# Eight late modulation blocks: from TensorE products to VectorE products with a TensorE sum over partitions

## The reference, cut to what matters

```
mod = silu(cond) @ w_ada + b_ada              # (1024) @ (1024 x 6144), for each of 2 conditioning vectors
sh1, sc1, g1, sh2, sc2, g2 = split(mod, 6)
h   = LN0(x) * (1 + sc1) + sh1                # needs the first third of mod
qkv, gates = h @ w_in                         # 1024 x 6656
x   = LN1(alpha * x + g1 * (merged @ w_o))    # needs the rest of mod, much later
```

## Time and profile before

| | |
|---|---|
| median of 3 runs | 1319.49 us (1319.38 to 1319.76) |
| profiled execution: its own time | 1320.33 us |
| profiled execution: span in the trace | 1317.9 us |
| TensorE busy | 1245.7 us (95% of the span) |
| VectorE busy | 947.4 us (72%) |
| ScalarE busy | 657.6 us (50%) |
| GpSimd busy | 235.2 us (18%) |
| granted TensorE clock, mean | 0.977 of full |

### The profile page before, as it was taken

How to read it: one execution, slowest core, us unless ns; L and a number is a source line. 1 busy time by engine, 2 the same in 40 slices (tenths; PEclk the granted TensorE clock), 3 DMA queues, 4 the chain that set the end, 5 groups by cost and what they waited for, 6 DMA issues and landing times.

```text
span 1317.9 us, 20584 instructions
## 1 busy us (share of the span) xinstructions
PE 1245.7 (95%) x6739; PEld 1009.7 (77%) x6739; DVE 947.4 (72%) x1714; ACT 657.6 (50%) x1043; POOL 235.2 (18%) x347
## 2 busy tenths in 40 slices
PE   7999999999999899998998999997899999999994
PEld 4677777778888799887876788784688888888862
DVE  5665531848461789888877524788999999999967
ACT  1522222232222688776763212224588888888843
POOL 0024441021242000011111001101131112112111
PEclk9999999999999999998998999997999999999997
DMA  9988995572655476532004533537999999999955
GB/s 349 281 299 276 289 290 217 167 238 82 221 168 207 164 232 218 182 140 81 25 24 128 183 131 105 203 144 263 322 387 374 372 389 381 384 384 377 376 218 119
DMA packets 152835, 309.46 MB, mean 235 GB/s; under 512 B 20700, under 2 KB 31516, under 8 KB 152760
## 3 DMA queue, kind: packets, MB, share of 16 engines
q1 hardware_dynamic: 122456, 233.24, 49.6%
q0 software_dynamic: 24384, 70.00, 17.4%
q10 hardware_dynamic: 5920, 5.24, 1.3%
HBM read 259.24 MB, written 61.24 MB: 243 GB/s over the span
## 4 chain that ended last, share of the span: by engine, by line
PE 81%; DVE 11%; issue 3%; DMA 2%; ACT 2%; SPq 1%; POOL 0%; DVEq 0%; ACTq 0%; POOLq 0%
PE psum_pair L1804 9%; PE psum_pair L1806 8%; PE psum_pair L1805 8%; PE psum_pair L1904 6%; PE psum_pair L2096 5%; PE psum_pair L2098 5%; PE psum_pair L2097 5%; PE psum_pair L1971 4%; PE psum_pair L1915 4%; PE psum_pair L1972 4%; PE psum_pair L1973 4%; PE psum_pair L1930 3%; PE psum_pair L2111 3%; PE psum_pair L2113 3%; PE psum_pair L2112 3%
## 5 line engine op out<-in xcount | busy, mean ns | idle before, releaser
L1804 PE MATMUL psum_pair<-w_parts,h_hi 128*128 128x512 f32 x520 | 206.5, 397 | 3.0 <-DVE h_lo L1313 3.0
L1806 PE MATMUL psum_pair<-w_parts,h_lo 128*128 128x512 f32 x520 | 203.4, 391 | 0.0
L1805 PE MATMUL psum_pair<-w_parts,h_hi 128*128 128x512 f32 x520 | 203.2, 391 | 0.0
L1164 DVE TENSOR_TENSOR w_parts<-w_raw,w_parts 128x1024 fp32r<-128x1024 f32 x72 | 83.4, 1220 | 97.3 <-ACT w_parts L878 96.8
L1018 ACT ACTIVATE p_unnormed<-psum_pair,minus_max 128x640 f32<-128x640 f32 (+1 forms) x160 | 113.4, 711 | 59.1 <-DVE minus_max L1391 58.9
L1391 DVE TENSOR_REDUCE minus_max<-psum_pair 128x1 f32<-128x640 f32 (+1 forms) x160 | 111.7, 715 | 22.6 <-PE psum_pair L1904 20.5
L1904 PE MATMUL psum_pair<-k_bundle,q_bundle 128*128 128x320 f32 (+1 forms) x576 | 115.7, 326 | 12.2 <-ACT p_unnormed L1018 10.8
L1804 PEld LDWEIGHTS psum_pair<-w_parts,h_hi 128*128 128x128 f32 x520 | 98.0, 188 | 25.1 <-issue 5.6
L1806 PEld LDWEIGHTS psum_pair<-w_parts,h_lo 128*128 128x128 f32 x520 | 98.0, 189 | 21.0
L1805 PEld LDWEIGHTS psum_pair<-w_parts,h_hi 128*128 128x128 f32 x520 | 98.2, 189 | 19.6
L1904 PEld LDWEIGHTS psum_pair<-k_bundle,q_bundle 128*128 128x128 f32 x576 | 86.2, 190 | 27.1 <-issue 24.8
(11 more groups left out here) (363 smaller groups left out, 2666.0 us busy)
## 6 DMA issues: line engine op xcount, KB each, us to landing
w_raw<-in_w_gate_up SPq DMA_DIRECT2D x76, 512.0 KB, 11.0
w_raw_c<-in_w_gate_up SPq DMA_DIRECT2D x72, 512.0 KB
w_raw_b<-in_w_down SPq DMA_DIRECT2D x72, 512.0 KB
w_raw<-in_w_in SPq DMA_DIRECT2D x52, 512.0 KB, 11.1
ada_raw<-in_w_ada SPq DMA_DIRECT2D x32, 512.0 KB, 9.3
k_transposed<-turned_staging POOLq DMA_DIRECT2D x48, 256.0 KB, 7.5
k_bundle<-k_transposed SPq DMA_DIRECT2D x14, 768.0 KB, 8.1
q_transposed<-turned_staging POOLq DMA_DIRECT2D x40, 256.0 KB, 6.3
```

The costliest lines, as they stand in the source:

```text
L1164: dve.tensor_tensor(w_parts[b % 2][:, 1, c], w_raw[:, c], w_parts[b % 2][:, 0, c].bitcast(F32), ALU.subtract).then_inc(lo_done, 1)
L1804: pe.matmul(out, a_hi, hi, start=kk == 0, stop=False)
L1805: pe.matmul(out, a_hi, lo, start=False, stop=False)
L1806: return pe.matmul(out, a_lo, hi, start=False, stop=kk == KD - 1)
```

## The change

The eight late `ada` units become two sums (after blocks 6 and 11). Their products are taken by VectorE, piece by piece: 32 pieces of 512 KB (`late_products`), each of four instructions on 128 x 512 values, which add up in `ada_acc`, four accumulators with two conditioning vectors each. TensorE multiplies the finished accumulators with a one-hot operand (`one_row`), which only sums over the partitions. The pieces are spread over blocks 3 to 11 as 3, 6, 6, 1, 1, 3, 5, 5, 2 (`LATE_CHUNKS`); pieces 0 to 15 make the first sum, 16 to 31 the second. Within a block, piece j of `count` is done at the end of VectorE's work for unit `j * 5 // count`. The ring of raw pieces shrinks from four places of a whole unit to two single pieces: SyncE issues piece m + 2 when VectorE has used piece m, behind the weights of its loop's turn. Pieces 0, 4, 8 and 12 of each sixteen belong to accumulator 0 and so on; the first two instructions of the first four pieces of each sixteen are plain products (`tensor_scalar`), all others are `scalar_tensor_tensor`, product and sum.

```diff
--- before.py
+++ after.py
@@ -204,21 +204,29 @@
 
         def ada_place(ci, c):
 
-            if ci < 4:
-                return ada_early[:, ci % 2, c], ada_early_in[ci % 2][c], 16 * (ci // 2 + 1)
-            return ada_ring[:, c], ada_in[c], 16 * (ci - 3)
+            return ada_early[:, ci % 2, c], ada_early_in[ci % 2][c], 16 * (ci // 2 + 1)
 
         KINDS = ["q", "q", "k", "k", "v", "v", "bq", "bq", "bkv", "g", "g", "g", "g"]
+        LATE_CHUNKS = {3: 3, 4: 6, 5: 6, 6: 1, 7: 1, 8: 3, 9: 5, 10: 5, 11: 2}
+        SUM_UNITS = {6: 7, 11: 11}
         units = []
         for b in range(NB - 6):
             _, i = blocks[b]
             if i == 2:
                 units += [("ck", None, 0, NT), ("ck", None, 1, NT), ("cbk", None, 0, NT)]
             units += [(KINDS[i], b, i, tt) for tt in range(NT)]
-            if b < N_ADA - 4:
-                units.append(("ada", -1, 4 + b, 0))
+            if b in SUM_UNITS:
+                units.append(("ada", -1, SUM_UNITS[b], 0))
         units = [("ada", -1, ci, 0) for ci in range(4)] + units
         N_EARLY = 4
+        late_of = {i: [] for i in range(len(units))}
+        m = 0
+        for b, count in LATE_CHUNKS.items():
+            of_block = [i for i, u in enumerate(units) if u[1] == b]
+            for j in range(count):
+                late_of[of_block[j * NT // count]].append(m)
+                m += 1
+        N_LATE = m
 
 
         pj_no, n = {}, 0
@@ -308,8 +316,9 @@
         vst_total = list(count)
 
         ada_early_in = [[sem(f"ada_early_in{i}_{c}") for c in range(NC_CH)] for i in range(2)]
-        ada_in = [sem(f"ada_in{c}") for c in range(NC_CH)]
+        ada_in = [sem(f"ada_in{c}") for c in range(2)]
         ada_used = sem("ada_raw_used")
+        acc_used = sem("ada_products_summed")
         mod_summed = sem("mod_summed")
         early_done = sem("picks_and_turned_bias_built")
         mod_done = sem("mod_columns_done")
@@ -327,7 +336,8 @@
         s3a = ExitStack()
         bundles = [(0, h) for h in range(A_HEADS)] + [(1, g) for g in range(B_KV)]
         sr = ExitStack()
-        ada_ring = sb("ada_raw", [P, NC_CH, 2, CW], F32, sr)
+        ada_ring = sb("ada_raw", [P, 2, 2, CW], F32, sr)
+        ada_acc = sb("ada_products", [P, 4, 2, CW], F32, sr)
         sr.close()
         qtb = [sb("q_bundle0", [P, REP, NT * P], F32R, s3a)]
         ktb = [sb("k_bundle0", [P, 2, 2, KCOL], F32R, s3a)]
@@ -338,6 +348,7 @@
         h_hi = sb("h_hi", [P, KD, NT * P], F32R, s12)
         h_lo = sb("h_lo", [P, KD, NT * P], F32R, s12)
         mod_parts = sb("mod_parts", [P, 2, CW], F32, s12)
+        one_row = mod_parts[:, 0, 0:34]
         cond_cols = sb("cond_columns", [P, KD, 32], F32, s12)
         bias12 = sb("ada_bias", [N_ADA, CW], F32, s12)
         cache = sb("cache_k", [P, D + B_KV * HD], F32, s12)
@@ -751,12 +762,14 @@
             def ada_weights(ci):
                 if 2 <= ci < 4:
                     sp.wait_ge(pj_ready, pj_no[ada_unit[ci - 2]] + 1)
-                if ci > 4:
-                    sp.wait_ge(ada_used, ci - 4)
                 for c in range(NC_CH):
                     dst, done, _ = ada_place(ci, c)
-                    src = ada_chunk(ci, c) if ci < 4 else ada_chunk(4 * (ci // 4) + c, ci % 4)
-                    sp.dma_start(dst, src).then_inc(done, 16)
+                    sp.dma_start(dst, ada_chunk(ci, c)).then_inc(done, 16)
+
+            def late_chunk(m):
+                if m >= 2:
+                    sp.wait_ge(ada_used, m - 1)
+                sp.dma_start(ada_ring[:, m % 2], ada_chunk(4 + 4 * (m // 16) + m % 4, m // 4 % 4)).then_inc(ada_in[m % 2], 16)
 
             for tt in range(NT):
                 src = t["x_prompt"][0] if tt == PROMPT else t["x_sample"][0, tt * P:(tt + 1) * P]
@@ -778,9 +791,15 @@
                 sp.dma_start(dst, t["ln2_b"][0:1, :].to_broadcast([P, D])).then_inc(out_cleared, 16)
             weights(1)
             for b in range(2, NB - 4):
-                if b - 2 < N_ADA - 4:
-                    ada_weights(b + 2)
                 weights(b)
+                if b == min(LATE_CHUNKS) + 1:
+                    late_chunk(0)
+                    late_chunk(1)
+                for i, u in enumerate(units):
+                    if u[1] == b - 2:
+                        for m in late_of[i]:
+                            if m + 2 < N_LATE:
+                                late_chunk(m + 2)
                 if b == 2:
                     sp.wait_ge(h_done, KD)
                     sp.wait_ge(cache_in, 112)
@@ -1268,7 +1287,7 @@
                 elif ci % 4 == 3:
                     r = ci // 4 - 1
                     dve.wait_ge(cache_in, 112 + 16 * (N_ADA - 4))
-                    dve.wait_ge(ada_used, ci - 3)
+                    dve.wait_ge(acc_used, r + 1)
                     dve.tensor_tensor(mst[:, r], mod_sum(r), bias_late[:, r], ALU.add).then_inc(mod_summed, 1)
 
 
@@ -1303,6 +1322,26 @@
                 dve.tensor_copy(h_mod[:, k], turned(n)[:, 0:NT * P]).then_inc(tr_free[n % 2], 1)
             for i in range(N_EARLY):
                 after(i)
+            link(dve.memset(one_row, 0.0))
+            link(dve.memset(one_row[:, 1:2], 1.0))
+
+            def late_products(m):
+                g, pair_of_k = m % 4, m // 4 % 4
+                dve.wait_ge(ada_in[m % 2], 16 * (m // 2 + 1))
+                if m == 16:
+                    dve.wait_ge(acc_used, 1)
+                for k in range(2):
+                    for s in range(2):
+                        acc, c = ada_acc[:, g, s], cond_t[:, 2 * pair_of_k + k, s:s + 1]
+                        if k == 0 and pair_of_k == 0:
+                            last = dve.tensor_scalar(acc, ada_ring[:, m % 2, k], c, None, ALU.mult)
+                        else:
+                            last = dve.scalar_tensor_tensor(acc, ada_ring[:, m % 2, k], c, acc, ALU.mult, ALU.add)
+                    if k == 0:
+                        link(last)
+                last.then_inc(ada_used, 1)
+                dve.wait_ge(ada_used, m + 1)
+
             for c in range(NC_CH):
                 dve.wait_ge(hi_done, c + 1)
                 dve.tensor_tensor(w_parts[0][:, 1, c], w_raw[:, c], w_parts[0][:, 0, c].bitcast(F32),
@@ -1322,6 +1361,8 @@
                     gain_tables()
                 if i - 2 >= N_EARLY:
                     after(i - 2)
+                for m in late_of[i]:
+                    late_products(m)
             after(len(units) - 2)
             after(len(units) - 1)
 
@@ -1769,14 +1810,13 @@
                 if b is None:
                     return
                 if kind == "ada" and ci >= 4:
-                    for k in range(2):
+                    r = ci // 4 - 1
+                    pe.wait_ge(ada_used, 16 * (r + 1))
+                    for s in range(2):
                         for g in range(4):
-                            src, done, value = ada_place(ci, g)
-                            if k == 0:
-                                pe.wait_ge(done, value)
-                            last = pe.matmul(mod_sum(ci // 4 - 1)[32 * g:32 * g + 32], cond_cols[:, 2 * (ci % 4) + k], src[:, k],
-                                             start=ci % 4 == 0 and k == 0, stop=ci % 4 == 3 and k == 1)
-                    last.then_inc(ada_used, 1)
+                            last = pe.matmul(mod_sum(r)[32 * g:32 * g + 32], one_row[:, 1 - s:33 - s], ada_acc[:, g, s],
+                                             start=s == 0, stop=s == 1)
+                    last.then_inc(acc_used, 1)
                     return
                 n = pj_no[i]
                 wait_bank(n)
@@ -2239,7 +2279,7 @@
                 if i == last_g:
                     for s in range(TST):
                         pool.wait_ge(tst_st[s], tst_total[s])
-                    pool.wait_ge(ada_used, N_ADA - 4)
+                    pool.wait_ge(acc_used, 2)
                     load_qk(pool, 0, first_in)
                     load_v(pool, 0, first_in)
             after(len(units) - 2)
```

## The result

The kernel after takes 1342.19 us in the median (1339.77 to 1347.39, four runs), the kernel before 1319.62 us in the same session: ratio 1.0173, 95% interval 1.0153 to 1.0194. It is slower, as forecast, but by 22.6 us where 10.8 were forecast, and it lies above the range. The profiled execution took 1347.39 us, its span is 1345.0 (before: 1317.9).

What follows compares the result with a forecast made beforehand. The prediction took TensorE to set the projection's pace, with VectorE's slack uneven. Its terms, -12.3 + 9.4 + 3.95 + 9.55 + 0.2 = +10.8 us, gave 1331.1 us profiled, 1330.3 on the median; range 1314 to 1338.

Steps and rivals of the forecast that it cites:

- Six units leave TensorE: Projection: eight late units go and two sums come, 6 x 2.05 = 12.3 us gained, all on the path.
- Block 8: Block 8: three pieces in units 0, 1 and 3 exceed VectorE's slack, so TensorE waits 3.95 us.
- The places named: Projection: TensorE idle about 9 us in block 6, 4 in 8, 9 to 10 in 10; none in 0 to 5, 7, 9, 11.
- the small things: Two memsets ahead of block 0 cost 0.2 us; SyncE's weights and GpSimd's wait for the second sum cost 0.
- The rival that held landings to be free: Projection: pieces land in 6.2 us or less throughout, sum +0.65, 1320.1 us; chance 0.20.
- A piece of four two-input products: VectorE: four instructions at 0.605 us with two waits of 0.12, 2.66 us a piece.
- the cheap piece: VectorE: a piece with two plain products, taken at 0.45 us each, costs 2.3 us; eight pieces are of this kind.
- Blocks 9 and 10: Block 9's landings leave VectorE a lag of 7.95 us; with block 10's pieces TensorE waits 9.55 us.
- block 6's landing: Blocks 4 and 5, ahead of block 6: five rounds of landings taken as 11, 8 and three of 5.5 us, 35.5 in all.
- a lag of 6.7: Block 6: VectorE ready for its first unit after 58.8 us instead of 52.1, 6.7 us late.
- Block 6 costs 9.4: Block 6: its own piece, 2.7 us, and the 6.7 us inherited from blocks 4 and 5 cost 9.4 us.
- the last rival: Projection: ring far behind, block 6's lag 12 us, pieces 2.9, clock might fall; +19.7, 1339.2 us; chance 0.14.

Runs made afterwards that it cites:

- the products alone: The kernel after with all 128 products, but only pieces 0 and 1 loaded and used again, so no product waits: 1319.25 us, ratio 0.9999.
- e6: The kernel after with SyncE issuing pieces 5 and 6 ahead of the weights of block 6: 1344.42 us, ratio 1.0186.
- e10: The kernel after with ScalarE issuing the loads of pieces 2 to 31 in its own queue: 1351.73 us, ratio 1.0236.
- e8: The kernel after with block 8's pieces moved to block 7 and four of block 10's to blocks 7 and 11: 1348.06 us, ratio 1.0213.
- e9: The kernel after with the first sixteen pieces moved to blocks 1 to 5: 1333.44 us, ratio 1.0104.
- e5: The kernel after with pieces moved: none in blocks 6 and 8, one in 10, the rest in 1 to 5, 7, 9, 11: 1333.35 us, ratio 1.0104.

## Why the prediction was wrong

**Right.** *Six units leave TensorE*: 12.3 forecast, 11.7 measured, the sum 1.92. *Block 8*: 3.95 forecast, 3.6 of idle time, 4.2 in the table with what follows the stalls. The places named were the places found; no other block stalls more than before, and the small things cost nothing that can be seen. The rival that held landings to be free (1320.1) is within a microsecond of the products alone (1319.25), in part by luck: it gave blocks 6, 8 and 10 2.7, 3.95 and 6.1 us, where the table has 4.1, 4.2 and 3.8.

**A little off.** A piece of four two-input products is 2.87 us, not 2.66: they run at 0.70 us from start to start where I took 0.605 from two neighbours with no wait between them. The plain products run at 0.40 from start to start (0.87 for two, with a last one of 0.48), so the cheap piece is the 2.3 forecast. The Trainium skill, VectorE: DVE Perf Modes, section "The perf-mode tier table", puts `tensor_scalar` on fp32 in SBUF at twice the rate of `tensor_tensor`; here 0.40 against the 0.60 of a `tensor_tensor` is 1.5 times, against the 0.70 of the product and sum 1.75 times.

*Blocks 9 and 10*, 9.55 forecast, look exact beside the 9.8 us of idle time, but the forecast was of all that VectorE's lag costs there, and that is more than idle time (below): 12.8 us in the table. An estimate from the 0.21 us that each of the nine pieces in the two blocks is dearer gives 1.9 of the 3.3 us between them.

**The step that failed** is block 6's landing: "I take 11 for the round behind the weights of block 6", "8 for the one behind block 7's and 5.5 for the three others", giving "a lag of 6.7" and "Block 6 costs 9.4". The four later rounds were not judged too low: their pieces land in 3.7 to 5.5 us. The first was: 22.8 us. The stores' load and the 2 MB ahead in the queue come together there: without the 2 MB ahead (e6) it took 12.3 us, in a queue of its own (e10) 13.9. I had a row for each alone, 17.3 us for a piece with its three fellows beside the stores and 10.5 for weights without stores, and took nearly the smaller one for the case in which both apply. The lag came out at 15.4 instead of 6.7. The block's stalls grew by 16.8 - 1.23 = 15.6 us, and with the slower matmuls in and behind it the table has 20.6 us where 9.4 were forecast. In the products alone, where no piece is waited for, it is 4.1.

**The term that was not in the sum** is the clock. I mentioned it in the last rival only, as something that "might fall for a while" if the ring fell far behind. It fell after each of the three stalls of over 4 us and cost 1.4 + 2.1 + 1.9 = 5.4 us. But these three do not weigh the same. From 235 to 275 us and from 370 to 413 us VectorE's timeline has no idle time, so within blocks 6 and 10 it is VectorE that sets when TensorE's next turn can start. A matmul at half rate ahead of such a turn only takes the place of idle time: without the 1.4 us the stalls that follow in block 6 would have been longer by as much, and so for the 1.9 in block 10. Only the 2.1 us behind block 6's last stall, with no wait after them, are a price of the clock itself. In the prediction's own terms block 6 cost 15.6 + 1.4 = 17.0 us instead of 9.4, block 10 9.8 + 1.9 = 11.7 instead of 9.55, and the clock 2.1 instead of nothing.

Either way of sorting gives -12.3 + 15.6 + 3.6 + 9.8 + 5.4 = +22.1. That this is near the 22.6 between the medians is luck: the stalls are those of the profiled execution, the slowest of the four, whose total grew by 27.1 us. There the time from the projection's first matmul to attention grew by 26.7. The 4.6 us left are 0.6 that the six units gave less than forecast, 0.8 in block 0, and some 3 in slower restarts: the first turn and the first matmul behind each of the eleven stalls.

The last rival, a ring far behind, was the right mechanism: it had a lag of 12 and 1339.2 us, and it named the clock. It got 0.14 because I judged the landing behind the weights by its own block rather than by that of the stores.

**What stays open.** Each experiment's profile is of one execution. With two places, the first piece behind the weights of block 6 landed after 22.8 us in the kernel after, 24.3 in e8, 22.6 in e9, 20.2 in e5 and, with the products left out, 14.7; no run shows what decides between these. Nor does one show why stalls of 2.2 to 3.9 us sometimes brought the clock down and sometimes did not.

## What to carry over

Work moved to an engine with idle time is free only if three things fit at each place: its price in that engine's slack before the next deadline (blocks 6, 8 and 10 had too little), its input landed by then, and nobody waiting for its result at once (the piece ahead of the sum). A ring needs enough places to keep its user at work while one landing is out; behind the large transfers of its queue two were too few here and cost 14 to 23 us against four; another order in the queue did not make up for it, and another queue did so only for a third, and only with the pieces spread. And a stall is to be priced with what follows it: in these runs one of over 4 us brought 0.7 to 2.4 us at the lower clock, which is a loss of its own only where no later wait for the same engine would have taken that time anyway.
